# One encoder layer on one core: which v rows VectorE adds, where tile 0 is routed, and which rows are loaded again

## What is computed

```python
mod = (jax.nn.silu(c) @ lp['w_ada'] + lp['b_ada'])[:, None, :]
sh1, sc1, g1, sh2, sc2, g2 = jnp.split(mod, 6, axis=-1)
h = rmsnorm(x, lp['norm1']) * (1.0 + sc1) + sh1
... = jnp.split(h @ lp['w_in'], [OFF_Z, OFF_A, OFF_B, OFF_QB, OFF_KB, OFF_VB], axis=-1)
o_a, conv_new, s_new = gdn_mixer(qkv_a, z_a, a_a, b_a, conv_buf, s0, lp, ...)
o_b = diff_attn_prompt(q, k_new, v_new, rel_table, lam)
...
mixed = jnp.concatenate([o_a, o_b], axis=-1)
x = x + g1 * (mixed @ lp['w_out'])
h2 = rmsnorm(x, lp['norm2']) * (1.0 + sc2) + sh2
x = x + g2 * peer(h2, lp)
y = rmsnorm(x, final_norm)

def peer(x, lp):                     # 8 heads, 16 experts each: 128 rows per token
    qh = x @ w_q                     # w_q: 1024 x 2048
    sc = einsum(qh, sub_keys)        # 128 keys per half
    ...                              # top 16 of each half, top 16 of the 256 sums
    gate = jax.nn.softmax(top_s)
    u = jnp.take(u_tab, eidx)        # 16384 x 1024
    act = jax.nn.gelu(einsum(u, x))
    vv = jnp.take(v_tab, eidx)       # 16384 x 1024
    return einsum(gate * act, vv)
```

## Time and profile before

| | |
|---|---|
| time before, median of 3 runs | 4339.26 us (4335.96 to 4350.27) |
| the profiled execution, its own time | 4341.6 us |
| its span | 4339.9 us |
| mean granted clock of TensorE | 0.907 |
| PE busy | 3391.8 us (78%) |
| DVE busy | 2489.9 us (57%) |
| POOL busy | 2309.2 us (53%) |
| ACT busy | 1106.3 us (25%) |
| moved by DMA | 1308.12 MB, mean 301 GB/s |

### The profile page before, as it was taken

The page is one execution under the profiler, slowest core; times in us unless marked ns, Lnnn a source line. Parts: engine busy times, 40 slices in busy tenths (PEclk is TensorE's granted clock), DMA queues, the critical chain, the costliest instruction groups (busy, mean ns, idle before and its releaser), DMA issues.

```text
span 4339.9 us, 37765 instructions
## 1 busy us (share of the span) xinstructions
PE 3391.8 (78%) x11402; PEld 1785.9 (41%) x11402; DVE 2489.9 (57%) x5734; ACT 1106.3 (25%) x2931; POOL 2309.2 (53%) x2237
## 2 busy tenths in 40 slices
PE   6797877638888779987986789787697788778755
PEld 1343764335555334433553344335253344235222
DVE  0132644356888766546775577654756646745653
ACT  1122334212221244112332345322211121121111
POOL 0000310006666756676777676675766666666674
PEclk9899988869999889998998899998899899899898
DMA  9322211049888989999999999999999999999996
GB/s 363 132 106 100 103 60 56 29 149 356 317 322 321 364 314 368 401 374 359 339 365 355 375 350 339 347 341 367 335 376 371 365 388 370 361 384 360 359 355 263
DMA packets 387978, 1308.12 MB, mean 301 GB/s; under 512 B 51348, under 2 KB 55684, under 8 KB 385735
## 3 DMA queue, kind: packets, MB, share of 16 engines
q0 software_dynamic: 309808, 1127.00, 69.5%
q1 hardware_dynamic: 74904, 157.12, 9.9%
q10 hardware_dynamic: 3072, 21.66, 1.3%
HBM read 1270.94 MB, written 38.99 MB: 302 GB/s over the span
## 4 chain that ended last, share of the span: by engine, by line
PE 33%; POOL 13%; issue 12%; DMA 11%; DVE 8%; ACT 2%; another core or an unknown queue 1%; SPq 0%; DVEq 0%; ACTq 0%; POOLq 0%
PE PS L1986 21%; DMA ubuf<-in_peer_u,idx 8%; POOL vbuf L1870 7%; POOL ubuf L1867 6%; PE PS L1655 5%; DVE ubuf L2032 3%; PE PS L2310 2%; PE PS L1376 1%; PE PS L1312 1%; PE PS L2307 1%; DMA ckeys<-rest_scratch 1%; PE PS L1641 1%; ACT diag L1941 1%; PE PS L1348 0%
## 5 line engine op out<-in xcount | busy, mean ns | idle before, releaser
L1986 PE MATMUL PS<-vbuf,diag 128*128 128x512 f32 x3936 | 1979.7, 644 | 537.6 <-issue 247.2
L1870 POOL DMA_INDIRECT vbuf<-in_peer_v,idx x1024 | 1079.8, 1054 | 733.1 <-PE PS L1986 368.3
L1986 PEld LDWEIGHTS PS<-vbuf,diag 128*128 128x128 f32 x3936 | 766.1, 206 | 1488.2 <-issue 1174.9
L1867 POOL DMA_INDIRECT ubuf<-in_peer_u,idx x1024 | 1074.3, 1049 | 389.0 <-issue 301.7
L2032 DVE SCALAR_TENSOR_TENSOR ubuf<-ubuf,PS 128x1024 f32<-128x1024 f32 x544 | 662.9, 1220 | 560.3 <-DMA ubuf<-in_peer_u,idx 414.9
L2032 DVE SCALAR_TENSOR_TENSOR ubuf<-ubuf,h2e 128x1024 f32<-128x1024 f32 x512 | 624.6, 1224 | 393.4 <-DMA ubuf<-in_peer_u,idx 339.5
L1951 ACT ACTIVATE acts<-dots 128x2 f32<-128x2 f32 x528 | 107.1, 203 | 2013.5 <-DVE ubuf L2032 1207.7
L1941 ACT ACTIVATE diag<-ident,coef 128x128 f32<-128x128 f32 x984 | 339.1, 387 | 26.7 <-PE PS L1986 21.8
L1655 PEld LDWEIGHTS PS<-h2T,wq 128*128 128x128 f32 x2304 | 290.2, 194 | 96.5 <-issue 84.8
L1655 PE MATMUL PS<-h2T,wq 128*128 128x128 f32 x2304 | 292.9, 277 | 9.6 <-ACT h2T L1595 8.5
L405 PE MATMUL PS<-w_in_sb,hT 128*128 128x512 f32 (+1 forms) x640 | 252.8, 554 | 4.0 <-DVE hT L426 2.8
(11 more groups left out here) (428 smaller groups left out, 3434.7 us busy)
## 6 DMA issues: line engine op xcount, KB each, us to landing
wada<-in_w_ada SPq DMA_DIRECT2D x12, 2048.0 KB, 18.6
wq<-in_peer_wq SPq DMA_DIRECT2D x8, 2048.0 KB, 11.4
ubuf<-in_peer_u,idx POOLq DMA_INDIRECT x1024
vbuf<-in_peer_v,idx POOLq DMA_INDIRECT x1024
w_in_sb<-in_w_in ACTq DMA_DIRECT2D x8, 1796.0 KB, 10.4
wst<-in_w_in SPq DMA_DIRECT2D x7, 2048.0 KB
sh<-pre_scratch SPq DMA_DIRECT2D x15, 768.0 KB, 5.7
wout<-in_w_out SPq DMA_DIRECT2D x2, 4096.0 KB, 19.0
```

The source lines that it names most:

```text
L1867: pool.indirect_dma_start(out=g["ubuf"][:, c % RU, :], out_offset=None, in_=d["peer_u"][0], in_offset=bass.IndirectOffsetOnAxis(ap=at, axi ...
L1870: pool.indirect_dma_start(out=g["vbuf"][:, c % RV_, :], out_offset=None, in_=d["peer_v"][0], in_offset=bass.IndirectOffsetOnAxis(ap=at, ax ...
L1986: last = pe.matmul(PS[:, h, :], g["diag"][:, (at - 1) % DIAGS, :], g["vbuf"][:, c % RV_, h * 512:(h + 1) * 512], start=(n == 0), stop=(n = ...
```

## The change

Six things, in the order of the diff. (1) `condition` loads the four vectors as rows (72 in all, 128 wide) and turns them on TensorE; w_in is loaded by column groups from the sixth group of w_ada on, and each group of products in `project` waits for its own. (2) `EVERY` picks every second slot beside projection and every fourth from 427 to 640; the first choice falls on even positions. (3) Tile 0 is routed in `attend_first`, from after its x1 on, in a row of written positions of its own (`sync_of_one`), with two buffers for the blocks of wq and PSUM banks 0 and 1; the stream's first routing stage begins with tile 1 at slot 4 in steps of 30.5 and loads keys, rows and wq itself. (4) h2 of tiles 5 to 7 is neither stored nor loaded: ScalarE copies it from `h2r` into PSUM, and SP waits for that before it reads the next x1. (5) `final_norm` is loaded once, into a tensor of its own. (6) Routing of tiles 5 to 8 starts five (later four) slots later; some tensors share memory.

```diff
+            for name in ("c_prompt", "c_sample", "b_ada", "norm1"):
+                rows = d[name][0, :].rearrange("(k p) -> k p", p=P)
+                sp.dma_start(vecs[row:row + rows.shape[0], :], rows).then_inc(ld_v, 16)
...
+            def columns_of_w_in(n):
+                cols = slice(n * GC, min((n + 1) * GC, IN_COLS))
+                act.dma_start(g["w_in"][:, :, cols], wi[:, :, cols]).then_inc(g["ld_win"][n], 16)
...
-                if 2 <= n < 2 + DC:
-                    act.dma_start(g["w_in"][:, n - 2, :], wi[:, n - 2, :]).then_inc(g["ld_win"], 16)
+                if n >= 5:
+                    columns_of_w_in(n - 5)
+            columns_of_w_in(7)
...
+            pe.transpose(PS[:, 3, 0:VECS], vecs[:, :], g["ident"][0:VECS, 0:VECS]).then_inc(v_psum, 1)
...
+            dve.tensor_copy(cT[:, :], PS[:, 3, 0:VECS]).then_inc(v_cols, 1)
...
+                    pe.wait_ge(g["ld_win"][n], 16)
...
-            pe.wait_ge(g["ld_win"], 16 * DC)
...
-ROUTE_STEP, ROUTE_LONG = 31.5, 54
+ROUTE_FROM, ROUTE_STEP, ROUTE_LONG = 4, 30.5, 52.5
 PROJECT_AT, DELTA_AT, ATTEND_AT, ROUTE_AT = 145, 292, 427, 604
-EVERY = ((PROJECT_AT, DELTA_AT, 4), (DELTA_AT, ATTEND_AT, 8), (ATTEND_AT, ROUTE_AT, 8))
+EVERY = ((PROJECT_AT, DELTA_AT, 2), (DELTA_AT, ATTEND_AT, 8), (ATTEND_AT, NSLOT * FRONT, 4))
...
-    return c % NSLOT > 2 * LAG and any(a <= c < b and c % every == 1 for a, b, every in EVERY)
+    return c % NSLOT > 2 * LAG and any(a <= c < b and c % every == 0 for a, b, every in EVERY)
...
+    def first_loads(self, sp, blocks=4):
+        kv = self.d["peer_keys"][0].rearrange("h two n c -> n (h two) c")
+        sp.dma_start(self.sc[:, :, :], kv).then_inc(self.r["key_in"], 16)
+        self.rows_of(sp, 0)
+        for b in range(blocks):
+            self.load_weights(sp, b)
+
+    def load_weights(self, sp, b):
+        wv = self.d["peer_wq"][0].rearrange("(k p) c -> p k c", p=P)
+        at = self.wq[:, b % 2, :, :] if self.streamed else self.wq[:, :, b * 512:(b + 1) * 512]
+        sp.dma_start(at, wv[:, :, b * 512:(b + 1) * 512]).then_inc(self.r[f"wq{b}"], 16)
+
+    def sync_of_one(self, sp, stored):
+
+        r, (rt, w0, w1) = self.r, self.routes[0]
...
+        yield 0
+        self.first_loads(sp, 2)
+        yield stored
+        sp.dma_start(self.h2r[:, :], self.g["x1_scratch"][rt]).then_inc(r["x1_in"], 16)
+        yield at(15)
+        sp.wait_ge(r["h2_ready"], rt + 1)
+        sp.dma_start(self.g["h2_scratch"][rt], self.h2r[:, :]).then_inc(r["stored"], 16)
+        for b in (2, 3):
+            yield at(31 + 10 * (b - 2))
+            sp.wait_ge(r["q_psum"], 4 * rt + b - 1)
+            self.load_weights(sp, b)
+        yield at(114)
+        sp.wait_ge(r["stored"], 16 * (rt + 1))
+        sp.wait_ge(r["idx_ready"], rt + 1)
+        sp.wait_ge(r["gate_ready"], rt + 1)
...
+            if from_router(rt - 1):
+                sp.wait_ge(self.experts.f["h2_psum"], self.experts.in_psum_to(rt - 1))
             sp.dma_start(self.h2r[:, :], g["x1_scratch"][rt]).then_inc(r["x1_in"], 16)
...
+            if not from_router(rt):
+                sp.dma_start(g["h2_scratch"][rt], self.h2r[:, :]).then_inc(r["stored"], 16)
...
+def from_router(t):
+
+    return FRONT <= t < NT
+
+
+def kept_rows(t):
+
+    return sum(not from_router(u) for u in range(t + 1))
...
+    def h2_loads(self, t):
+
+        return sum(64 if group(u) else 16 for u in range(t % 2, t + 1, 2) if not from_router(u))
...
-            pool.wait_ge(r["stored"], 16 * (t + 1))
+            if from_router(t):
+                return
+            pool.wait_ge(r["stored"], 16 * kept_rows(t))
...
+                some(pool, f["square"], t)
                 pool.dma_start(g["x1e"][:, :], g["x1_scratch"][t]).then_inc(f["x1e_in"], 16)
-                yield end + 15
-                pool.wait_ge(f["square"], t + 1)
-                pool.dma_start(g["x1e"][:, :], d["final_norm"].partition_broadcast(P)).then_inc(f["fin_in"], 16)
+                if t == 0:
+                    yield end + 15
+                    pool.dma_start(g["fnorm"][:, :], d["final_norm"].partition_broadcast(P)).then_inc(f["fin_in"], 16)
...
+                if from_router(t):
+                    act.wait_ge(self.r["h2_ready"], t + 1)
+                    rows = self.router.h2r[:, :]
...
-        stage(0, lambda m: Router(nc, g, d, m, 0, [(0, -NSLOT, 0)] + [(t, ROUTE_STEP * (t - 1), ROUTE_STEP * (t - 1) + ROUTE_LONG) for t in range(1, FRONT)]))
+        stage(0, lambda m: Router(nc, g, d, m, 1, [(t, ROUTE_FROM + ROUTE_STEP * (t - 1), ROUTE_FROM + ROUTE_STEP * (t - 1) + ROUTE_LONG) for t in range(1, FRONT)]))
...
-        stage(0, lambda m: Router(nc, g, d, m, 1, [(t, max(ROUTE_AT, number(t - 1, 0)), number(t, 0)) for t in steady]))
+        stage(0, lambda m: Router(nc, g, d, m, 2, [(t, max(ROUTE_AT + 5, number(t - 1, 4)), number(t, 0)) for t in steady]))
...
+        stored = a.at(H - 1, 38.6)
+        route = (0, stored + 5, stored + 115)
+        router = Router(nc, g, d, m, 0, [route], ((0, 1), (0,), (1,)), streamed=True)
...
+            a.sync(sp, [router.sync_of_one(sp, stored)])
...
+            weave(Between(None, 0), *a.scalar(act), *router.scalar(act))
...
+            weave(Between(None, 0), *a.tensor(pe), *router.tensor(pe))
...
+            weave(Between(None, 0), *a.vector(dve), *router.vector(dve))
```

More of the change, by code:

```diff
@@ L1622, in route_tensor @@
             for b in range(4):
-                some(pe, r["key_sb"], 4 * self.stage + b - 1 if b >= 2 else 0)
+                some(pe, r["key_sb"], 4 * self.stage + b - len(self.SBANK) + 1 if b >= len(self.SBANK) else 0)
                 for j in range(4):
-                    last = pe.transpose(PS[:, self.SBANK[b % 2], j * P:(j + 1) * P], keys[:, 4 * b + j, :], ident[:, :])
+                    last = pe.transpose(PS[:, self.SBANK[b % len(self.SBANK)], j * P:(j + 1) * P], keys[:, 4 * b + j, :], ident[:, :])
                 last.then_inc(r["key_ps"], 1)
@@ L1824, in on_dve, with in_psum_to @@
         return sum(on_dve(x) for x in range(c + 1))
+    def h2_loads(self, t):
+        return sum(64 if group(u) else 16 for u in range(t % 2, t + 1, 2) if not from_router(u))
+    def in_psum_to(self, t):
+        return sum(in_psum(u) for u in range(t + 1))
     def v_free(self, eng, c):
@@ L2021, in slot @@
             if n == 0:
-                dve.wait_ge(self.h2_in[t % 2], 16 * (t // 2) + (64 if group(t) else 16))
+                if not from_router(t):
+                    dve.wait_ge(self.h2_in[t % 2], self.h2_loads(t))
                 if group(t):
@@ L2027, in slot @@
                 if in_psum(t):
-                    dve.wait_ge(f["h2_psum"], sum(in_psum(u) for u in range(t + 1)))
+                    dve.wait_ge(f["h2_psum"], self.in_psum_to(t))
             c = number(t, lo + n)
@@ L3016, in build @@
             g["w_in"] = me.sb("w_in_sb", [P, DC, IN_COLS])
-            g["ld_win"] = me.sem("ld_win")
+            g["ld_win"] = [me.sem(f"ld_win{n}") for n in range(8)]
             condition(nc, g, d)
             project(nc, g, d)
+        g["idx"] = m.sb("idx", [P, HELD, NSLOT], U32)
+        g["gate"] = m.sb("gate", [P, HELD, NSLOT])
+        g["route"] = Router.sems(m)
         with ExitStack() as mid, Memory(nc, mid) as mm:
```

120 lines of the change are left out of this document (60 added, 60 removed).

## The result

The changed kernel takes 4303.3 us (median of 6 runs, 4298.63 to 4310.48) against 4334.6 of the kernel before: a ratio of 0.9925, 95% interval 0.9906 to 0.9944. That is some 32 us less (24 to 41). The forecast was 98.5 less; the time lies inside the stated range, near rival (a), and the gain is a third of the one forecast. The profiled execution took 4306.13 us, its span is 4304.4.

A forecast was written before the change was run, and what follows sets the result against it. The prediction saw a serial head, then a gather stream paced by DMA at 2.914 us a slot. Its terms summed to -98.5, taken from the profiled 4341.6 us: 4243 us, with a range of 4195 to 4315.

The forecast's parts named there:

- rival (a): Thinner cover: routing lengthens attention by 55, loads cost 32, v rows cost 10, the transition gives nothing; 4312 us, chance 0.12.
- empty opening: Stream's opening: with tile 0 routed beside attention, the 97.7 us without slots nearly vanish; -94 us (-98 to -85).
- attention longer: Attention before the stream: tile 0's routing beside it brings TensorE to 156 us, at 0.82 busy 190; +29 us (0 to +98).
- loads among the first gathers: First slots: routing tiles 1 to 4 loads some 11 MB after the gathers start; +25 us (0 to 32).
- head: Start to project: vectors loaded as rows and w_in by column groups let weights land earlier; -15 us (-22 to 0).
- fewer reloads: final_norm loaded once, h2 of tiles 5 to 7 not reloaded: 7.3 MB less at 369 GB/s; -16 us (-20 to -8).
- tail: End of the kernel: VectorE no longer waits 2.70 us for final_norm; -1.5 us.
- v rows beside projection: Stream beside projection: 33 more v rows on VectorE lift DMA share from 0.83 towards 1.00; -10 us (-21 to +42).
- v rows beside attention: Slots 427 to 604: 20 more v rows on VectorE lift DMA share from 0.95 towards 1.00; -8 us (-29 to +26).
- passage from tile 4 to 5: Between tiles 4 and 5: route starts five slots later, keys get 14.5 us more; -8 us (-20 to +12).
- (c): Stream: every added v row holds a GpSimd gather 1.285 us, 78 us in all; 4347 us, no change, chance 0.04.
- (b): Attention and v-row stretches: VectorE becomes the gate, its added 56.5 and 78 us are the price; 4375 us, slower, chance 0.05.

The follow-up runs named there:

- e2: The changed kernel with VectorE adding the v rows of the kernel before (72 slots in place of 133): 0.9941 of the kernel before, median 4328.45 us.

## Why the prediction was right or wrong

| term | predicted | measured |
|---|---|---|
| empty opening | -94 | -95.7 |
| attention longer | +29 | +70.3 |
| loads among the first gathers | +25 | +18.3 |
| head | -15 | -14.0 at project's first product, -16.5 at attention's first load |
| fewer reloads | -16 | 0, within the scatter |
| tail | -1.5 | -8.0 in this pair |
| v rows beside projection | -10 | -5.5 (-8 to -15 by e2, and not kept to slot 1024) |
| v rows beside attention | -8 | -0.8 |
| passage from tile 4 to 5 | -8 | -0.9 |

**Right**: what bounded the kernel, the gap, its price and that the first gather would come 3 us after the opening (2.0). The head, whose two mechanisms both show in the time line; the wait for the first rows of x grew from 15.38 to 19.20 us, which is the term that was set against them. The loads among the first gathers: 18 us, DMA-bound as argued, shown by the run that takes them away again. The v rows beside projection: the sign and the place are right, though the whole time shows no gain from the rows. DMA at 0.83 rose to 0.86 and not to 1.00. TensorE there waits 30.2 us for ScalarE, with the remaining v rows behind it, and waited 27.8 before, so that these waits hold the share down is the likely cause, not a shown one. The kernel before (1442 to 1913), then the changed one (1418 to 1900):

```profile
PE PS L2324 <- ACT cS L2241: 27.8, 7, 5.8
```

```profile
PE PS L2399 <- ACT cS L2316: 30.2, 6, 7.3
```

**Wrong, and by far the most**: the step "156/0.82 is 190, so +29 us". It failed twice. (1) Its list of what SP is held up by had the waits for h2 and the query blocks, and left out the first loads at the start of attention, 6.3 MB ahead of a qk load that was needed at once: 18 us, shown by putting them behind it. (2) It took a rate of work from another stretch and spread the routing evenly over 161 us. In the stretch 965 to 1445 at least 74 slots lie between the end of a tile's routing and its use; attention of one tile after another is a chain through the engines, and the routing's work fell into it in lumps, 24.7 of TensorE's 40.1 us into the second stretch and 41.1 of VectorE's 53.4 into the last two; more work for TensorE in the second and for VectorE in the third shows at 0.8 and 0.7 of its length. That is 52 us in place of 29. How much of the 52 the lower clock of the last two stretches adds (0.80 and 0.71, 0.90 and 0.82 before) is not separated. The measured 70 lies inside the bounds of 0 and 98, on the side that I did not take.

**Wrong**: the step "7.3 MB at 369 GB/s, most lies where DMA sets the pace". A share of 0.97 was read as a full queue. The stretch from slot 640 on carried 3.7 MB more at the same length with a higher rate, so it had room for them: priced 16 in all, worth 0. The first slots show what full means, 388 GB/s at 1.00. The Trainium skill (DMA: Bandwidth & Descriptors, Issuing engines are not separate DMA queues) says that transfers of all issuing engines interleave on the same 16 DMA engines; the first slots agree, where SP's weights slow the gathers by 18 us, while in the steady stretch a share of 0.97 left room.

**Wrong**: the step "0.95 to 1.00 is 29 us; -8", for the v rows beside attention. It turned a DMA share that isn't full into a gain without showing that TensorE's time was what emptied it. The row to ask was among TensorE's waits, not GpSimd's: 53.9 us for the diagonals. Taking some 25 us of work from TensorE there left the stretch as long as it was. The passage is the same mistake with less in it: slots 608 to 624 gained 14 us and the next sixteen gave 13 back.

The tail is not settled: VectorE's 2.70 us wait for final_norm is gone, but the stretch from slot 1024 to the end took 124.5 to 130.3 us in the runs, 125.3 with the reloads back, so no more than that is the change's.

Of the rivals, (a) came nearest in time (4312), for the mechanism that it names and one that it doesn't, and in part by luck: its 55 was 70, its 32 was 18, and its v rows, which were to cost 10, cost nothing. That the time lies in the stated range is no more than this, since the range took (a) in. (c), GpSimd held by v rows, would have needed gathers of over 1.38 us beside attention; they went from 1.13 to 1.15 (203.95/177). (b) needed VectorE near 95%; it was at 66%. The stand of ScalarE for h2 four slots into tiles 5 to 7 did not come: its copies there (L2021) waited for nothing.

## What to carry to other kernels

Before work is moved beside a stage, ask whether that stage is a chain or a stream: in a stream it may vanish into slack, in a chain it is exposed by a good part of its length on whichever engine it lands, and a test with the work doubled, read by the busy time that it really added, shows what more work costs there. Follow a moved load to the next load in the same queue, because the first thing that it delays may belong to the stage that should have covered it. A share of busy DMA under 1.00 says neither that more bytes cost time nor that fewer win it, until the same stretch has been seen with more in it.

## What had not been expected of the hardware

TensorE's granted clock fell where work was taken from it. Slots 208 to 288, beside the projection: the kernel before, then the changed kernel, then the run with the v rows of before:

```profile
1668.00:1913.00 245.00, 236.48 (x604) 108.97 (x603) 138.44 (x242) 63.48 (x163) 174.47 (x163) 0.97 1.00 387
```

```profile
1639.00:1884.00 245.00, 218.53 (x543) 101.94 (x544) 159.20 (x259) 57.62 (x145) 175.13 (x163) 0.94 1.00 382
```

```profile
1653.00:1903.00 250.00, 238.66 (x606) 110.06 (x605) 138.03 (x241) 63.76 (x165) 180.56 (x162) 0.97 0.99 378
```

The products of the v rows in the same stretch, with the other group that grew slower, the products of 128x8, before and changed (behind the bar busy us and the mean ns of one, then the idle time before them):

```profile
L1986 PE MATMUL PS<-vbuf,diag 128*128 128x512 f32 x252 | 121.2, 610 | 6.8 <-DVE ye L2052 6.4 <-issue 0.3
L2295 PE MATMUL PS<-wab,hT 128*128 128x8 f32 x64 | 7.4, 256 | 0.0
```

```profile
L2060 PE MATMUL PS<-vbuf,diag 128*128 128x512 f32 x184 | 94.6, 642 | 18.9 <-DVE ye L2127 9.5 <-issue 8.3 <-ACT diag L2010 1.1
L2370 PE MATMUL PS<-wab,hT 128*128 128x8 f32 x64 | 10.5, 296 | 4.3 <-issue 4.3
```

At 121.2/252 = 0.481 us each, 68 records less would free 32.7 us; 26.6 came, and the 64 products of 128x8, the same in both, took 3.1 us more. So some 9 of the 32.7 us came back, over a quarter, in this pair of profiles. The granted clock is a mean of two levels, 1.2 and 2.4 GHz; it went from 0.97 to 0.94 here (0.92 to 0.95 in the eleven other runs with the changed rows) and back to 0.97 when the rows came back, with TensorE busy 97%, 89% and 95% of the stretch. The Trainium skill (TensorE: Matmul & The Clock Gate, What's actually happening) says that the clock follows how busy the array has been; these rows agree. Part of what is taken from TensorE is so given back by its clock.
